# Turning the last chunk of a mixed activation in VectorE blocks and through DRAM instead of with TensorE transposes

## The reference, cut to what matters

```python
D_MODEL = 2048; SEQ = 256; D_FF = 4 * D_MODEL
def second_block(x, c, w_ada, ...):
    cs = silu(c)
    mod = cs @ w_ada + b_ada                      # 6 x 2048 numbers
    sh1, sc1, gt1, sh2, sc2, gt2 = split(mod, 6)
    h = rmsnorm(x, g_pre_mix) * (1 + sc1) + sh1
    ..., ga, gb = split(h @ w_in)
    ya = moba_attention(...) @ w_moba_out
    yb = dsa_attention(...) @ w_dsa_out
    y = (sigmoid(ga) * ya + sigmoid(gb) * yb) @ w_o
    x = x + gt1 * rmsnorm(y, g_post_mix)
    h = rmsnorm(x, g_pre_ffn) * (1 + sc2) + sh2
    f = square(relu(h @ w_ff1)) @ w_ff2
    return x + gt2 * rmsnorm(f, g_post_ffn)
```

## Time and profile before

| | |
|---|---|
| median of 3 runs | 1775.48 us (1774.52 to 1777.9) |
| the profiled execution | 1778.26 us, of which 1776.6 us are the span from the first to the last instruction |
| PE busy | 1757.2 us (99%) |
| DVE busy | 1267.0 us (71%) |
| ACT busy | 883.4 us (50%) |
| POOL busy | 203.0 us (11%) |
| TensorE's granted clock, mean | 0.998 |
| moved by DMA | 454.29 MB, mean 256 GB/s |

### The profile page before, as it was taken

How to read it: one execution, slowest core, us unless ns; L and a number is a source line. 1 busy time by engine, 2 the same in 40 slices (tenths; PEclk the granted TensorE clock), 3 DMA queues, 4 the chain that set the end, 5 groups by cost and what they waited for, 6 DMA issues and landing times.

```text
span 1776.6 us, 24966 instructions
## 1 busy us (share of the span) xinstructions
PE 1757.2 (99%) x8130; PEld 1444.4 (81%) x8130; DVE 1267.0 (71%) x1649; ACT 883.4 (50%) x1235; POOL 203.0 (11%) x377
## 2 busy tenths in 40 slices
PE   9999999999999999999999999999999999999998
PEld 7777778887888888788888878888888888888886
DVE  5787779777988788677678768777775655455455
ACT  6866684545444344434435445444444444444443
POOL 1011101010334332400010101000000000000000
PEclk9999999999999999999999999999999999999999
DMA  9887778555798898798988957999998775555554
GB/s 358 267 301 247 253 248 322 199 165 171 239 274 290 276 293 266 243 301 303 328 292 298 314 186 256 317 314 310 313 296 240 233 221 194 190 195 193 191 192 139
DMA packets 201711, 454.29 MB, mean 256 GB/s; under 512 B 20160, under 2 KB 31408, under 8 KB 201264
## 3 DMA queue, kind: packets, MB, share of 16 engines
q1 hardware_dynamic: 168080, 343.28, 59.5%
q0 software_dynamic: 33424, 110.19, 18.7%
q10 hardware_dynamic: 144, 0.03, 0.0%
HBM read 434.03 MB, written 12.06 MB: 251 GB/s over the span
## 4 chain that ended last, share of the span: by engine, by line
PE 87%; DMA 5%; DVE 4%; ACT 1%; issue 1%; POOL 0%; SPq 0%; DVEq 0%; ACTq 0%; POOLq 0%
PE bank L1678 28%; PE bank L1680 27%; PE bank L1679 27%; DMA ada_raw<-in_w_ada 3%; DMA raw<-in_w_in_a 2%; DVE w_lo L1065 2%; DVE acc_a L1072 1%; PE bank L1842 1%; PE bank L1724 1%; PE bank L1832 0%; PE bank L1943 0%; DMA rope_ab<-rot 0%; POOL sums_r L394 0%; ACT w_hi L653 0%; PE bank L1823 0%
## 5 line engine op out<-in xcount | busy, mean ns | idle before, releaser
L1065 DVE TENSOR_TENSOR w_lo<-raw,w_hi 128x1024 fp32r<-128x1024 f32 x605 | 730.6, 1213 | 421.2 <-ACT w_hi L653 420.2
L653 ACT ACTIVATE w_hi<-raw 128x1024 fp32r<-128x1024 f32 x605 | 634.2, 1050 | 754.8 <-PE bank L1680 627.8
L1678 PE MATMUL bank<-w_hi,h_hi 128*128 128x512 f32 x2272 | 891.8, 393 | 5.0 <-DVE w_lo L1065 2.8
L1680 PE MATMUL bank<-w_hi,h_lo 128*128 128x512 f32 x2272 | 884.8, 389 | 0.0
L1679 PE MATMUL bank<-w_lo,h_hi 128*128 128x512 f32 x2272 | 884.5, 389 | 0.0
L1678 PEld LDWEIGHTS bank<-w_hi,h_hi 128*128 128x128 f32 x2272 | 426.6, 188 | 99.4 <-issue 8.5
L1680 PEld LDWEIGHTS bank<-w_hi,h_lo 128*128 128x128 f32 x2272 | 426.5, 188 | 89.4
L1679 PEld LDWEIGHTS bank<-w_lo,h_hi 128*128 128x128 f32 x2272 | 426.8, 188 | 86.4
L540 POOL DMA_DIRECT2D ada_raw<-in_w_ada x160 | 85.2, 533 | 764.1 <-DVE acc_a L1072 543.2
L1072 DVE SCALAR_TENSOR_TENSOR acc_a<-ada_raw,cond,acc_a 128x1024 f32<-128x1024 f32 x112 | 143.3, 1279 | 21.6 <-DMA ada_raw<-in_w_ada 21.6
L1072 DVE SCALAR_TENSOR_TENSOR acc_b<-ada_raw,cond,acc_b 128x1024 f32<-128x1024 f32 x48 | 61.4, 1279 | 6.5 <-DMA ada_raw<-in_w_ada 6.5
(11 more groups left out here) (211 smaller groups left out, 932.3 us busy)
## 6 DMA issues: line engine op xcount, KB each, us to landing
raw<-in_w_ff SPq DMA_DIRECT2D x256, 512.0 KB, 4.6
raw<-in_w_in SPq DMA_DIRECT2D x176, 512.0 KB, 5.0
ada_raw<-in_w_ada POOLq DMA_DIRECT2D x160, 512.0 KB, 6.2
raw<-in_w_in_a SPq DMA_DIRECT2D x69, 512.0 KB, 5.7
ada_more<-in_w_ada POOLq DMA_DIRECT2D x32, 512.0 KB, 6.3
raw<-in_w_out_a SPq DMA_DIRECT2D x32, 512.0 KB, 5.8
raw<-in_w_o SPq DMA_DIRECT2D x32, 512.0 KB, 5.4
raw<-in_w_moba SPq DMA_DIRECT2D x16, 512.0 KB, 5.7
```

The lines of the kernel that those rows point to most:

```text
L653: act.activation(used(w_hi, turn, s), used(raw, turn, s), ACT.Copy).then_inc(hi_ready, 1)
L1065: dve.tensor_tensor(used(w_lo, turn, s), used(raw, turn, s), used(w_hi, turn, s).bitcast(F32), ALU.subtract).then_inc(lo_ready, 1)
L1678: pe.matmul(out_ap, hi, rhs_hi, start=start, stop=False)
L1680: return pe.matmul(out_ap, lo, rhs_hi, start=False, stop=stop)
```

## The change

Chunk 3 of the mixed y is treated like the other three, with POOL in SP's place. DVE runs `block_y` for it, POOL writes `gate_b` to a fourth part of `y_home` and reads it back in four pieces, and ACT and DVE make units 6 and 7 of the activation with `round_y` and `low_y` in slot 4 instead of slot 2. The 8 PE transposes and the two ACT copies are gone. POOL's loads 146 to 159 are issued around the new DMAs: the write stands between loads 145 and 146, the four reads between 146 and 147.

```diff
-        y_home = nc.dram_tensor("y_home", (CHUNKS - 1, P, T * CH), F32, kind="Internal").ap()
+        y_home = nc.dram_tensor("y_home", (CHUNKS, P, T * CH), F32, kind="Internal").ap()
...
@@ gpsimd
-            load_tiles(140, SC2, 6, 10)
+            load_tiles(140, SC2, 6, 3)
+            pool.wait_ge(y_blocked, CHUNKS * T)
+            pool.dma_start(y_home[CHUNKS - 1, :, :], y_blk).then_inc(y_back_written, 16)
+            load_ada(146, 0, SC2, 9, 0)
+            last_blocks = y_home[CHUNKS - 1, :, :].rearrange("(i f) (j n) -> j f i n", i=QUADS, j=QUADS)
+            last_y = y_t[:, KT - 4:KT, :].rearrange("p b n -> p (b n)").rearrange("p (i n) -> p i n", i=QUADS)
+            pool.wait_ge(y_back_written, 16)
+            for j in range(QUADS):
+                pool.dma_start(last_y[j * QUAD:(j + 1) * QUAD], last_blocks[j]).then_inc(y_back_loaded, 16)
+            load_ada(147, 1, SC2, 9, 1)
+            load_tiles(148, SC2, 10, 6)
@@ scalar
-            def keep_last_y():
-                for t in range(T):
-                    act.wait_ge(y_turned, t + 1)
-                    act.activation(y_t[:, KT - 4:KT, t * P:t * P + P], two(banks[TURNED + t][:, :], 4), ACT.Copy)\
-                        .then_inc(y_t_ready, 1)
...
-                    if n == 0 and s == 2:
-                        keep_last_y()
-                        act.wait_ge(y_t_ready, T)
+                    if n == 0 and s == 4:
+                        act.wait_ge(y_back_loaded, 16 * QUADS)
                         for k in (6, 7):
-                            round_h(y_t, k)
+                            round_y(k)
@@ vector
             gate_y(CHUNKS - 1)
+            block_y(CHUNKS - 1)
             dve.wait_ge(gain_ready, 4)
...
-                    if n == 0 and s == 2:
+                    if n == 0 and s == 4:
                         for k in (6, 7):
-                            low_h(y_t, k, UPT)
+                            low_y(k)
@@ tensor
-            def turn_last_y():
-                for t in range(T):
-                    pe.wait_ge(y_tok_ready, CHUNKS * T + t + 1)
-                    turn_rows(y_tok, t, 4, banks[TURNED + t], y_turned)
...
-                    if n == 0 and s == 1:
-                        turn_last_y()
```

More of the change, by code:

```diff
@@ L324, in two_block_kernel @@
         y_tok_ready = sem("y_tok_ready")
-        y_turned = sem("y_turned")
+        y_back_written = sem("y_back_written")
+        y_back_loaded = sem("y_back_loaded")
         y_summed = sem("y_summed")
@@ L329, in two_block_kernel @@
         y_loaded = sem("y_loaded")
-        y_t_ready = sem("y_t_ready")
         f_sq = sem("f_sq")
```

## The result

The changed kernel takes 1781.36 us (median of 7 runs, 1778.69 to 1783.61) where the kernel before took 1775.48 beside it (7 runs, 1773.7 to 1778.68): a ratio of 1.0036, 95% interval 1.0025 to 1.0046. It is slower by 5.9 us; 2.5 were forecast. Two later comparisons of the same pair gave 1.0027 (1.0017 to 1.0037) and 1.0037 (1.0026 to 1.0048).

What follows compares the result with a forecast made beforehand. It took the chain of loads and DVE steps to W22, not PE, as the bound; three paths delay step 147, taken as +2.5 us on 1775.48, giving 1778.0 us. Range 1775.0 to 1781.5, the forecast's own 1776.5 to 1779.0.

Steps and rivals of the forecast that it cites:

- the slack of 2.16 us at W22: First output turn: PE idles 0.33 and 1.83 us waiting for DVE, so 2.16 us of PE delay is absorbed.
- PE's big visible stall is not the price: Ahead of W6 PE stalls 3.9 us; after 0.88 and the slack 0.9 remains, 2.2 with lower clock, under 2.5.
- the slow return: Rival: write 8.1 and last read 7.6 us make step 147 6.0 us late, 1781.5 us; chance 0.30.
- Where step 147 comes out: First output turn: step 147 starts about 17.6 us after chunk 3's mixing, where it was 15.1.
- The three paths: To step 147: DVE's own order gives 987.9, chunk 3's return 987.3, load 147 986.8; the last to arrive counts.
- The block transposes' 1.3 us: On DVE after chunk 3's mixing: two added block transposes, 1.30 us, go on the chain in full.
- The write and the reads: Chunk 3's trip through DRAM: write lands in 6.6 us, reads in 5.1, chunk 3 back at 985.2.
- Load 147: the term that was mis-sized: Behind the four reads: load 147 issued at 980.6, takes 6.2 us, lands at 986.8, 1.5 us late.
- an aside: Within the slow return: load 147 alone brings that outcome if it takes 8.3 us from 980.6.
- Everything from there follows rigidly: After step 147: steps 149, 151, 153, 155, 158 and W22's release each come 2.5 us later.
- Its own signs: Right: PE idles 3 to 4 us before W6, write 6 to 7 us; wrong: lower clock beyond three us.
- What is removed is worth nothing: First output turn: dropping PE's 8 transposes gives back 0.88 us, which becomes idle time, worth 0.

Runs made afterwards that it cites:

- after_again: The changed kernel with no edit, timed and profiled again beside the kernel before: ratio 1.0027 (1.0017 to 1.0037), +4.8 us.
- trip_unwaited: Changed kernel, but units 6 and 7 made from chunk 2's data, so nothing waits for the return until the second output turn: ratio 1.0026, +4.2 us over before.
- write_only: Changed kernel without the four reads; units 6 and 7 made from chunk 2's data, so nothing waits for chunk 3: ratio 1.0008, +1.6 us over before.
- four_wide: As trip_unwaited, but each of the four reads takes 1 KB from each of all 128 partitions: ratio 1.0017, +2.8 us over the kernel before.
- plain_read: As trip_unwaited, but one 512 KB read in 4 KB rows replaces the four, blocks unsorted: ratio 1.0008 in both timings, +1.4 us over the kernel before.
- four_plain: As trip_unwaited, but the four reads of 32 partitions take whole 4 KB rows, blocks unsorted: ratios 1.0028 and 1.0022, +3.7 and +3.6 us over before.
- sort_in_write: Changed kernel with blocks sorted in four writes of 32 partitions and read back by one 512 KB read: ratio 1.0028, +4.8 us over the kernel before.

## Why the forecast was wrong, by its own steps

**The step that failed: the slack of 2.16 us at W22, and with it "PE's big visible stall is not the price".** The forecast took load 146's 8.88 us, step 147 at 15.1 us and PE's 2.16 us of slack as the kernel's. They were one execution's. In two more profiles the load takes 6.0 us, the step starts at 13.1 and 13.2, PE doesn't idle at W22, and the chain there is PE alone. Two things follow. The steps' chain starts from 13.1, not from 15.1, so its delay is 4.2 to 5.0 us and not 2.5. And what PE loses counts in full: the forecast's own terms for it (3.9 of stall, 1.3 for the lower clock, less 0.88) make +4.3 without the slack, where it had +2.2. Measured were 4.43 and 2.3 less 0.88 in after_again, 5.9 us, and the end was 5.9 late. The forecast gave the profile its due 2.8 us over the median and then took them off again at the end, without asking where they lay: 2.5 of them lay behind the mixing, 2.0 already at step 147. Against the exceptional execution the forecast's +2.5 is what the first pair of profiles shows (809.0 less 806.4, 2.6); against the usual one the same end is 5.2 us late.

**The number.** 1781.36 us lies outside the forecast's own 1776.5 to 1779.0, and near the 1781.5 that the slow return was given. That nearness is luck: write and last read took 11.5 us together (12.1 and 12.2 in the two other profiles), not the 13.3 of that rival.

**Where step 147 comes out: nearly right.** 17.6 us behind the mixing was forecast, 17.35 was measured, then 18.0 and 18.1. PE idle ahead of W6: 3.9 forecast, 3.7, 4.4 and 4.5 measured. The end point was sized well, if from terms that were off in both directions; the starting point wasn't.

**The three paths, in us behind the mixing.** DVE's own: step 146 starts at 12.2, and with 1.20, 1.14 and 1.29 step 147 would be free at 15.9 (forecast 17.7, since load 146 was given 8.9 us and took 7.1). The return: 17.35 (17.1). Load 147: 17.33 (16.6). So the order of the three was wrong: DVE's own path set nothing for step 147. It does set a floor for PE: the pair behind step 146 leaves PE idle for 1.28 to 1.48 us ahead of W6 even where nothing waits for the return and the reads are one or none, which the forecast didn't see. The block transposes' 1.3 us still count, since they stand at the head of the return.

**The write and the reads.** 6.6 and 5.1 us were taken; 3.4 and 8.05 came (8.7 and 8.8 for the last read in the two other profiles). The sum (11.7 against 11.5) was right by luck. For the write the rows of SP's writes were chosen, and the estimate of 3.2 us from the Trainium skill (DMA: Bandwidth & Descriptors, section Anatomy of one DMA, SWDGE (gpsimd) path) was set aside; the measured 3.4 agrees with the page. For the reads 5.1 was the row of 32 KB moves by the same engine, and SP's reads of the same size and shape, 6.1 to 7.6, would have been nearer.

**Load 147: the term that was mis-sized.** Forecast: issued 10.4 us behind the mixing, 6.2 us to land, as if its neighbours didn't touch it. Measured: issued at 7.9, 9.4 to 10.0 us to land. The rival "the return is slow" had an aside on it ("load 147 alone does it if it takes 8.3 us from 980.6"), which puts its landing at 18.7 us behind the mixing. The load took longer than that but was issued 2.5 us sooner, and landed at 17.3 to 17.9: neither the aside nor the main condition, 13.3 us for write and last read, was met.

**"Everything from there follows rigidly": half right.** trip_unwaited, with a stall of only 1.69 us at W6, keeps 4.2 us of loss over the loads. But from step 147 to step 158 it takes 39.8 to 43.5 us over the profiles, 41.7 to 42.3 in those of the kernel before, and in the changed kernel the steps are delayed again at step 150, by 0.5 to 1.5 us, behind PE.

**Its own signs.** It named as a sign of being wrong that PE runs at the lower clock for longer than three us, so that the chain goes over PE. That is what happened: 3.4 and twice 6.8 us. Of the signs of being right the stall ahead of W6 came (3.7 to 4.5 us against 3 to 4), PE's second, brief idle time at W22 in two profiles of three (0.61 and 0.27 us), and the write's 6 to 7 us didn't.

**What is removed is worth nothing**: right within what can be measured (-0.5 us), and 0.66 of the 0.88 us are seen again as idle time.

What stays open: why load 146 took 8.88 us once; how much of the time over many runs is the clock's, and how often the return and how often the loads set the end; what made load 147 slower in write_only; what one wide read with the wait kept would cost, since no run has just that; and how much of four_wide's time, between those of its neighbours, is its own. No version tried is faster than the kernel before; the best of those with a trip through DRAM both ways (plain_read) still loses 1.4 us by the means, and it doesn't even sort its blocks.

## What to carry to other kernels

Take a second and a third profile of the unchanged kernel before a term is built on one load's duration, and where the profiled execution lies above its median, find the place of the excess first. A slack that one profile shows is no cover: see whether the busiest engine idles at the same place in the others. Price a new DMA by what it does to those behind it while the engines are full: bytes, and also how many partitions each transfer reaches. When several paths end within a microsecond of one another, taking one away tells little; take both away, and look in each profile for the one that set the end.

## What the runs showed of the hardware that was not expected

- Full DMA engines don't move a fixed rate. With four 128 KB reads into 32 partitions each among 512 KB loads they moved 265 to 287 GB/s at a share of 0.98 to 1.04; with one read into 128 partitions, or four, 348 to 351.
- A write of 512 KB issued by POOL landed in 3.4 us in all three profiles of the changed kernel, one by SP in 2.9, where SP's writes in the y stage take 6.9.
- After 3.74 us of idle time PE's granted clock was 0.50 for 3.4 us; after 4.43, 4.52 (twice) and 6.14 us of it for 6.8 us. In all of them it fell before the first matmul behind the idle time. After 2.45 and 2.56 us it was 0.50 for 3.4 us in four_plain's two profiles, and after 2.31 us at W22 in trip_unwaited; after 0.3 to 1.9 us in these turns never. The idle time alone doesn't decide: near 729 us it stayed at 1.00 after 2.58 us in four_wide and after 3.16 us in sort_in_write.
- Runs of the unchanged kernel spread from 1771.2 to 1781.8 us. The stall near 729 us differs between executions, whatever the kernel: 1.5 to 3.7 us long over all profiles, with no stretch at the lower clock behind it in some of them and up to 6.8 us in others.
